# First feed-forward also by seven half-width products, experts' buffers given back in two parts, look-ahead limited to free buffers

## The reference

```python
D_FF = 2816
def swiglu(x, w_in, w_out):
    g, u = jnp.split(x @ w_in, 2, axis=-1)
    return (jax.nn.silu(g) * u) @ w_out

for layer in range(DEPTH_2):                       # 2 layers
    h = h + 0.5 * swiglu(rms_norm(h, ffn1_norm[layer]), ffn1_w_in[layer], ffn1_w_out[layer])
    ...                                            # layer 0: even mixer, layer 1: odd mixer
    h = h + 0.5 * swiglu(rms_norm(h, ffn2_norm[layer]), ffn2_w_in[layer], ffn2_w_out[layer])
return h[:, N_META:]
```

## Time and profile before

| | |
|---|---|
| median of three runs | 2871.68 us |
| profiled execution, its own time | 2872.69 us |
| its span, first to last instruction | 2870.9 us |
| TensorE busy | 2780.8 us (97%) |
| VectorE busy | 1139.5 us (40%) |
| first feed-forward, first product to the next stage's first | 1557.67 to 1804.63 us |
| second feed-forward | 2091.64 to 2321.58 us |
| third feed-forward | 2321.58 to 2544.69 us |

### The profile page before, as it was taken

How to read it: one execution, slowest core, us unless ns; L and a number is a source line. 1 busy time by engine, 2 the same in 40 slices (tenths; PEclk the granted TensorE clock), 3 DMA queues, 4 the chain that set the end, 5 groups by cost and what they waited for, 6 DMA issues and landing times.

```text
span 2870.9 us, 40516 instructions
## 1 busy us (share of the span) xinstructions
PE 2780.8 (97%) x16939; PEld 1908.7 (66%) x16940; DVE 1139.5 (40%) x2357; ACT 374.4 (13%) x772; POOL 28.5 (1%) x56
## 2 busy tenths in 40 slices
PE   8999999989999999999999999999999999998998
PEld 7977778833333333333335888777799999986998
DVE  2644441222222222222224110363377567635874
ACT  1132420200000000000002000112110010013100
POOL 0000000000000000000000000000000000000000
PEclk9999999999999999999999999999999999999999
DMA  5133234569999999999997333432244444442440
GB/s 211 62 105 118 88 138 153 199 236 424 429 428 429 429 428 428 429 428 428 429 429 312 139 140 147 160 118 88 74 156 163 147 147 154 170 150 81 150 174 16
DMA packets 50080, 655.32 MB, mean 228 GB/s; under 512 B 6016, under 2 KB 8208, under 8 KB 10880
## 3 DMA queue, kind: packets, MB, share of 16 engines
q1 hardware_dynamic: 45696, 642.90, 55.8%
q0 software_dynamic: 3104, 9.48, 1.0%
q10 hardware_dynamic: 1152, 1.05, 0.1%
HBM read 652.36 MB, written 1.05 MB: 228 GB/s over the span
## 4 chain that ended last, share of the span: by engine, by line
PE 84%; DMA 8%; DVE 5%; ACT 1%; issue 1%; PEldq 0%; DVEq 0%; PEld 0%; SPq 0%; ACTq 0%
PE bank L357 72%; DMA weight_ring<-weight_stream 8%; PE bank L1163 2%; PE bank L2169 1%; PE bank L2138 1%; DVE expert_hidden L2271 1%; DVE expert_hidden L2270 1%; PE bank L2160 1%; ACT expert_y_slots L2216 0%; DVE mlstm_qk L1536 0%; PE bank L3342 0%; PE bank L2874 0%; PE bank L3321 0%; PE bank L725 0%; PE bank L3189 0%
## 5 line engine op out<-in xcount | busy, mean ns | idle before, releaser
L357 PE MATMUL bank<-weight_ring,expert_x_slots_t 128*64 128x512 f32 x2048 | 459.8, 600 | 4.1 <-DMA weight_ring<-weight_stream 4.1
L357 PEld LDWEIGHTS bank<-weight_ring,expert_x_slots_t 128*64 128x64 f32 x2048 | 141.1, 138 | 319.9 <-issue 305.2
L357 PE MATMUL bank<-x,first_weight_ring 128*128 128x256 f32 x1376 | 317.4, 386 | 15.7 <-DMA first_weight_ring<-weight_stream 8.0
L357 PEld LDWEIGHTS bank<-x,first_weight_ring 128*128 128x128 f32 x1376 | 261.5, 193 | 59.2 <-issue 18.7
L357 PE MATMUL bank<-ffn_x_normed,weight_ring 128*128 128x136 f32 (+1 forms) x1440 | 243.2, 278 | 0.0
L357 PE MATMUL bank<-weight_ring,expert_hidden_slots_t 128*64 128x512 f32 x1024 | 225.2, 592 | 0.0
L357 PE MATMUL bank<-ffn_h,weight_ring 128*128 128x136 f32 (+2 forms) x1144 | 216.5, 315 | 8.7 <-DVE ffn_gate_pair L2585 8.2
L357 PEld LDWEIGHTS bank<-ffn_x_normed,weight_ring 128*128 128x128 f32 x1440 | 201.6, 191 | 0.2
L357 PEld LDWEIGHTS bank<-ffn_h,weight_ring 128*128 128x128 f32 x1144 | 178.9, 192 | 23.3 <-DVE ffn_gate_pair L2585 8.6
L2280 DVE TENSOR_TENSOR moe_rows<-moe_rows,bank 128x512 f32<-128x512 f32 x128 | 79.4, 682 | 269.1 <-PE bank L2169 269.1
L357 PEld LDWEIGHTS bank<-weight_ring,expert_hidden_slots_t 128*64 128x64 f32 x1024 | 73.4, 137 | 146.4 <-issue 123.2
(11 more groups left out here) (659 smaller groups left out, 3203.6 us busy)
## 6 DMA issues: line engine op xcount, KB each, us to landing
weight_ring<-weight_stream SPq DMA_DIRECT2D x276, 2048.0 KB, 15.2
first_weight_ring<-weight_stream SPq DMA_DIRECT2D x29, 2048.0 KB, 7.8
first_weight_ring<-weight_stream SPq DMA_DIRECT2D x4, 512.0 KB, 12.3
x<-x_t SPq DMA_DIRECT2D x2, 512.0 KB, 7.2
out_t<-x ACTq DMA_DIRECT2D x8, 128.0 KB, 2.0
c_ret_ret_q<-const_ret_q POOLq DMA_DIRECT2D x1, 544.0 KB, 5.2
c_ret_ret_k<-const_ret_k POOLq DMA_DIRECT2D x1, 544.0 KB, 5.9
c_odd_pool_inv<-const_pool_inv POOLq DMA_DIRECT2D x1, 544.0 KB, 3.8
```

Of the source, the lines that this page charges most:

```text
L357: ins = K.nc.tensor.matmul(out, lhsT, rhs, start=start, stop=stop, skip_group_check=shared)
```

## The change

1. The first feed-forward goes through `swiglu_pairs` too, with four plain pairs of columns (PLAIN_FIRST = 4, 64 full products) in place of two. The stream on the host is laid out to match, and `swiglu` goes. The layer norm becomes a function `last_norm` that `swiglu_pairs` calls after it has allocated its buffers.
2. The experts' buffers lie in two stacks. The one with the routing and the gathered inputs is given back ahead of the first feed-forward, the one with the experts' sum after the layer norm.
3. `add_weights` ends its look-ahead where the buffer of the next block is still in use at the end of the unit at hand: block b only goes ahead if block b-2 ends within that unit. All four feed-forwards use it.

The core of the diff:

```diff
+PLAIN_FIRST = 4
...
-    ffn("ffn1", 0)
+    ffn_pairs("ffn1", 0, PLAIN_FIRST)
...
 def norm_and_swiglu(K):
+    K.moe_early.close()
+    swiglu_pairs(K, "ffn1_norm_2", 0, normed_first=lambda xg: last_norm(K, xg))
+
+def last_norm(K, xg):
...
-        swiglu(K, "ffn1_norm_2", 0, xg)
+    K.moe_late.close()
...
     def add_weights(self, dve, upto):
-        while self.summed < len(self.blocks) and self.blocks[self.summed][1] < upto:
+        while self.summed < len(self.blocks) and self.blocks[self.summed][1] < upto + KP:
             b = self.summed
+            if b >= 2 and sum(self.blocks[b - 2][1:]) > upto:
+                return
...
-        plain_banks = ((3, 4), (5, 7))
+        plain_banks = ((3, 4), (5, 7), (0, 1), (3, 4))
...
         def _(pe):
-            for j in range(PLAIN):
+            for j in range(plain):
+                if j == 3:
+                    pe.wait_ge(*plain_free.take())
...
+                    if normed_first is not None and j == 1 and f == 0:
+                        rms.gather(pe)
             pe.wait_ge(*x_ready.take())
+            if plain > 2:
+                pe.wait_ge(*plain_free.take(2))
             for n in range(ins):
                 if n == 1:
-                    pe.wait_ge(*plain_free.take(PLAIN))
+                    pe.wait_ge(*plain_free.take(plain - 3 if plain > 2 else 2))
                 seven.tensor(pe, n, inputs)
...
         def _(dve):
-            rms.gained(dve, gain, layer, xg, t0)
+            if normed_first is None:
+                rms.gained(dve, gain, layer, xg, t0)
+            else:
+                seven.add_weights(dve, 0)
             rms.inverse_root(dve)
...
-                    seven.add_weights(dve, sum(seven.units[n]) + KP)
+                    seven.add_weights(dve, sum(seven.units[n]))
                     seven.combine(dve, n, o[:, :])
...
-            moe = ExitStack()
+            K.moe_late, K.moe_early = ExitStack(), ExitStack()
```

More of the change, by code:

```diff
@@ L2589, in end, with swiglu_pairs @@
         pe.wait_ge(*self.banks_free.take(2))
-def swiglu_pairs(K, gain, layer, last=False):
+def swiglu_pairs(K, gain, layer, last=False, normed_first=None):
     nc, block, bank = K.nc, K.block, K.bank
@@ L2658, in _ @@
             rms.scalar(act)
-            for j in range(PLAIN):
+            for j in range(plain):
                 act.wait_ge(*g_scaled.take())
-                act.activation(s[:, j, :], s[:, j, :], ACT.Silu).then_inc(*s_ready.post())
+                act.activation(s[:, j % 2, :], s[:, j % 2, :], ACT.Silu).then_inc(*s_ready.post())
             for q in range(0, ins, 2):
@@ L2687, in _, with scaled @@
[L2687 to L2690, removed]
+            def scaled(j):
+                dve.wait_ge(*gu_ready.take())
+                dve.tensor_tensor(out=s[:, j % 2, :], in0=bank[plain_banks[j][0]][:, 0:T], in1=rms.rstd[:, t0:T2], op=ALU.mult)\
+                   .then_inc(*g_scaled.post())
+                dve.wait_ge(*gu_ready.take())
+                dve.tensor_tensor(out=up[:, j % 2, :], in0=bank[plain_banks[j][1]][:, 0:T], in1=rms.rstd[:, t0:T2], op=ALU.mult)\
+                   .then_inc(*plain_free.post())
@@ L2692, in turn_over @@
             def turn_over(i):
-                dve.wait_ge(*h_mult.posted())
+                dve.wait_ge(*chain.posted())
                 seven.add_inputs(dve, h[:, 2 * i, lo], h[:, 2 * i, hi], h[:, 2 * i + 1, lo], h[:, 2 * i + 1, hi],
                                  h_sums[:, i, 0, :], h_sums[:, i, 1, :], h_sums[:, i, 2, :], h_ready)
[L2697 to L2706, removed]
+            def plain_pair(i):
+                dve.wait_ge(*plain_free.posted())
+                dve.wait_ge(*s_ready.take(2))
+                dve.tensor_tensor(out=h[:, 2 * i:2 * i + 2, :], in0=s[:, :, :], in1=up[:, :, :], op=ALU.mult).then_inc(*chain.post())
+                turn_over(i)
@@ new lines, in _ @@
+            if plain > 2:
+                scaled(0)
+                scaled(1)
+            dve.wait_ge(*rms.hn_ready.posted())
+            a, b = slice(0, DT // 2), slice(DT // 2, DT)
+            for part in (a, b):
+                dve.tensor_tensor(out=hn[:, part, :], in0=xg[:, part, :], in1=each, op=ALU.mult).then_inc(*chain.post())
+            dve.wait_ge(*chain.posted())
+            seven.add_inputs(dve, hn[:, a, lo], hn[:, a, hi], hn[:, b, lo], hn[:, b, hi], hn_sums[:, 0], hn_sums[:, 1], hn_sums[:, 2], x_ready)
@@ L3681, in build @@
         K.rms = RmsOfX(K, ctx)
-        with moe:
-            for s in STAGES[5:min(upto, 7)]:
-                s(K)
-        for s in STAGES[7:upto]:
+        for s in STAGES[5:upto]:
             s(K)
```

110 lines of the change are left out of this document (25 added, 85 removed).

## The result

The changed kernel takes 2842.57 us in the median of four runs (2829.44 to 2845.34), the kernel before 2871.62 us beside it: 0.9882 of it, 95% interval 0.9865 to 0.9899. That is 29 us less, within the range of 2834 to 2845, 4.6 us above the forecast of 2838.

What follows compares the result with a forecast made beforehand. TensorE bounds the kernel, in the first feed-forward by the number and price of its products. -23.6 - 8.3 - 2.1 = -34.0 us takes 2872.69 to 2838.7, from the median rounded 2838; own range 2834 to 2841, stretched to 2845.

Steps and rivals of the forecast that it cites:

- -25.2 -0.5 +2.1: First feed-forward: cheaper products, the wait between inputs and outputs gone, a longer end; together -23.6 us.
- The cover: First feed-forward: 64 plain products hide VectorE's first block, inverse root and normed input; least room 3.4 us.
- The rival of more than half a full product's price: First feed-forward: weight loads make 812 half-width products cost 0.38 us each, 120 us more, 2958; chance 0.02.
- VectorE as the bound: Rival, first feed-forward: VectorE's loop outgrows 13 us a pair, nine input pairs wait 17 us, 2855; chance 0.02.
- The circle of two engines: Second feed-forward, inputs to outputs: TensorE and VectorE wait for each other; removal saves 6.42 us plus 3.09 of lower clock.
- The new wait: Second feed-forward: TensorE waits about 1.2 us for the late block's sums, leaving net -8.3 us.
- The rival that the new wait costs as much as the old: Late block in second feed-forward, or tight bank in first, costs up to 9.5 us, up to 2847; chance 0.13.
- The reason given for taking only 1.2 us: After the third feed-forward's 1.94 us wait, four matmuls took 0.73 us, against 1.27 at the lower clock.
- Net about -2.1 us: Third feed-forward: the gap of 2.1 us between inputs and outputs goes, at most 0.1 us is left.
- all other stages keep their time: Stages outside the first three feed-forwards change by 0; moves over 1 us would show the prediction wrong.
- first rival: A wait in the second or first feed-forward replaces the removed one, up to 9.5 us, up to 2847; chance 0.13.
- Buffers: Experts' buffers in two parts: no instruction, no wait, no price of place, so nothing gained or lost.

Runs made afterwards that it cites:

- e4: The changed kernel with two plain pairs of columns in the first feed-forward in place of four: 2848.76 us, ratio 0.9915 to the kernel before.
- e2: The kernel before with only the limit on the look-ahead added: 2866.97 us, ratio 0.9974.
- e1: The changed kernel without the limit on the look-ahead: 2845.82 us, ratio 0.9906 to the kernel before.
- e3: The kernel before with only the experts' buffers in two stacks, given back in two parts: 2874.99 us, ratio 1.0001.
- e5: The changed kernel with seven unread products of constants filling TensorE's standstill at the end of the first three feed-forwards: 2839.05 us, ratio 0.9879.
- f2: The changed kernel with the filled standstills once more, on another chip: 2841.69 us, ratio 0.9877 to the kernel before.
- e0: The changed kernel run again with no edit: 2844.27 us, ratio 0.9896 to the kernel before.
- f1: The changed kernel a third time, unedited, on another chip: 2845.55 us, ratio 0.9896 to the kernel before.
- e8: The changed kernel with the first full block behind a short one cut into two of four sevens: 2838.16 us, ratio 0.9888 to the kernel before.
- f3: The changed kernel with the cut block once more, on another chip: 2837.68 us, ratio 0.9869 to the kernel before.

## Why the prediction was right, and where a step failed

**First feed-forward, right.** The forecast of -23.6 was -25.2 -0.5 +2.1; the rows give 1.622 us a seven and 4.59 us for the end, as the second feed-forward had them, and -23.67 in all. The cover held: no gap, and without it (e4) the stage loses 6.6 us. The rival of more than half a full product's price falls, since 1.622 / 7 = 0.232 us against 0.460. So does VectorE as the bound: it is busy 143.97 of 223.29 us, 64%, where the prediction said about three quarters.

**Second feed-forward, right.** The circle of two engines was the cause: the limit alone (e2) takes it away, -8.14, and without the limit (e1) it is back, +6.61. The new wait is 1.09 us for 1.2, and brings no lower clock. The rival that the new wait costs as much as the old falls with that. The reason given for taking only 1.2 us was weaker than it looked: the third's wait, which brought no lower clock in the one profile of before, came with it in e1 and e3 (1.9 us each; 224.79 us at 0.99, for 223.11 at 1.00).

**Third feed-forward: the mechanism was right, the term failed.** "Net about -2.1 us" holds where the clock stays up (-1.91 in e2, e5 and f2). In the changed kernel the stage gains 0.22, as 1.7 us are lost at its start.

**The step that failed: that all other stages keep their time.** The prediction said that it is wrong if others move by more than 1 us. The odd mixer moved by +5.15 to +5.26 us in all three profiles of the changed kernel (116.04, 116.06, 115.95 for 110.80), with the instructions of before at a lower clock. The forecast carried the lower clock only where a wait came or went; it took the clock of an untouched stage for granted. Without this loss and the third's 1.7 the profiled execution of e0 would be at 2845.98 - 5.24 - 1.7 = 2839.0 us; the forecast for a profiled execution was 2838.7.

**Luck in the number.** In the profiled run of the result the part ahead of the first feed-forward was 4.77 us shorter and hid most of the miss. It moved by more than 1 us too, and didn't repeat (1557.85 us in e0, 1558.11 in f1, 1557.67 before). In the first median one run of 2829.44 us helped: the three others took 2841.02 to 2845.34 us, and all eight later ones 2843.77 to 2846.51. Beside the kernel before, the later groups gave -30.4 and -30.1 us for the -34.0 of the sum. And 2842.57 us lies above the forecast's own range (2834 to 2841), in the part that the prediction left to its first rival, whose mechanism didn't come.

**Buffers, right:** 1.0001 (0.9990 to 1.0012).

**What stays open.** That the short standstill at a stage's end takes part in the lower clock behind it is shown by e5 and f2, and by the even mixer's first 10 us. What decides that it comes in one arrangement and not in another isn't: the kernel before, e1, e2, e3, e4, e8 and f3 are free of it at the third feed-forward's start with the same 1.6 us standstill ahead, and e8 and f3 are one program with two odd mixers. The moment at which the standstill falls is my guess; no run moved that alone.

## What to carry to other kernels

A price taken from the same tile shapes in another stage of the same trace held to 0.1 us over 23 us, and so did a wait worked out from when its producer can start. Look-ahead into a double buffer should stop where the buffer isn't free: an engine that waits in order for it blocks everything queued behind. Before a sum is closed, look at the granted clock of each stage that isn't touched: one that begins behind a short standstill moved by 5 us here without an edit. Filling that standstill with products of constants is a cheap test of it. It needn't be a gain: behind the first feed-forward it only moved the lower clock.

## What was not expected of the hardware

- A standstill of 1.6 us and one of 0.7 us, 1.2 us of work between them, were followed by the lower clock at the start of the third feed-forward (0.59 over 4.12 us) in all three profiles of the changed kernel, and in none of the seven of other kernels with the same standstills; the one of 6.40 us in e4 was followed by 0.74 over 6.52 us, and the wait of 1.09 us in the second feed-forward by none.
- The odd mixer takes 107.07 us at a clock of 1.00, 110.62 to 110.80 at 0.95, 111.47 to 111.97 at 0.94, 113.35 at 0.92 and 115.7 to 116.1 at 0.90, with the same work.
- The part ahead of the first feed-forward, with the same instructions in all kernels, wandered from 1552.90 to 1563.76 us between profiles, more than the odd mixer's whole loss; the four feed-forwards repeat to 0.1 us in the changed kernel's three profiles.
